# Streaming encoder block on 8 cores: normalisation of x, key products and pooling values in one stream

## The chip, the cores and the metric

The kernel runs on 8 cores of one Trainium2 chip. Each core computes one of the 8 sequences of the batch; the cores exchange nothing. The metric is the device time of the slowest core, in microseconds (us), as the median of several runs. Engines are called PE (TensorE, matrix products), ACT (ScalarE), DVE (VectorE), POOL (GpSimd) and SP (the queue that issues loads).

## The reference

Each core gets x (2048 rows of 1024) and puts 16 learned meta rows in front, so there are T = 2064 rows. Cut to what the change touches:

```
u  = rmsnorm(h, norm1_g)                       # h: meta rows and x
q, c, iq, ik, iw, pv, gates = split(u @ w_in)  # 512|128|256|32|8|512|2048 columns
c  = rmsnorm(c, kv_norm_g)                     # latent keys, 128 wide
attn = sparse_attention(q, iq, iw * IDX_SCALE, c, ik)   # top 256 keys by an index score
pool = multiscale_pool(pv)                     # 4 groups of 128 channels, windows 2, 4, 8, 16:
                                               # trailing mean minus the value, then w_pool, scale
merged = sigmoid(gA) * (attn @ w_a) + sigmoid(gB) * (pool @ w_b)
h  = h + merged @ w_out;  h = h + moe(rmsnorm(h, norm2_g));  out = rmsnorm(h)
```

All of the change lies in what is computed before the attention: u, c, iw, ik, iq, pv and the pooling.

## The kernel before, in words

The program is one list of operations for each engine, in the order in which the Python code calls `pg.op` and `pg.dma`. Every engine works off its own list strictly in that order. Each operation names the buffers that it reads and writes, and the class `Prog` turns these into waits on semaphores: nothing is reordered later, so the order of the calls is the order on each engine. The first stretch, up to the first `pg.barrier()`, is written as phases one behind the other.

1. **Norm of x** (loop over `tiles`: the meta rows, tile -1, then 16 tiles of 128 rows). SP loads a tile into one of four buffers. `rmsnorm_to_uT` squares and sums it on ACT (L433), takes the root on ACT (L436) and the reciprocal on DVE (L439), scales it on DVE (L440, into `xn`, two buffers), and transposes it on PE in 8 pieces (L449, PSUM banks 0 and 1). The copy of the transposed tile into `uT` (ACT, L457) is called one tile later, so ACT squares the next tile meanwhile.
2. **Key products** (`p2a_f1` and its two later parts, by tiles): PE multiplies `uT` of the tile by 136 columns of weights (8 matrix products, L522, banks 2 and 3): 128 latent keys and 8 index weights. ACT squares the keys (L529) and takes the root (L532); DVE does reciprocal, scaling and index weights (L535, L536, L541). One tile later PE transposes the keys (L547), and ACT copies them out (L552).
3. **Pooling values** (`p2b_pv(m)`, m = 3, 2, 1, 0): channel group m for the blocks of 16, 512, 512, 512 and 512 rows. One value group is 8 matrix products (L623) and one copy from PSUM to `pvT` on ACT (L582). The banks rotate over all 8.
4. **Pooling sums** (`p3_chain(g)`): g+1 steps of doubling. In each step POOL adds the first 1024 rows (L639) and DVE the rest (L642), and each half needs both halves of the step before; then DVE takes the mean minus the value (L652) with two short pieces for the first rows (L656, L659) into one of two buffers `dT`. `p3_chain(3)` is called after value group 2, `p3_chain(2)` after group 1.
5. **Index keys and queries** (`p2b_ik`, L592, 5 blocks; `p2b_iq`, L608, 12 groups of 8 products), each copied by ACT.
6. **Pooling products** (`p3_mm(g)`: 4 products, L667, and 4 copies on ACT, L671). `p3_chain(1)` needs the `dT` buffer that `p3_mm(3)` reads, and `p3_chain(0)` the one that `p3_mm(2)` reads; both products are called after all index products.

Then comes the barrier, on which all engines wait; behind it POOL issues the load of `w_uk` (the first L122 row after it) and clears buffers (L721), and the attention begins. What follows the barrier is the same in both kernels.

POOL's queue also fetches the weights, cast to bf16 on the way: `wsmall` (128 columns), `wsmall2` (8), `wik` three times (32 columns each, into three places side by side), `w_iq2` (256), `wslab` (512) and `wpool`, in this order, right at the start.

The lines that carry the order:

```
for j in tiles:                      # norm of x
    ...
    bk_ = rmsnorm_to_uT(xt4[k], [B('xt', k)], rows, col0, gbc[0], B('gbc', 0), j)
...
for j in tiles:                      # key products, after all tiles
    f2 = p2a_f1(j)
...
p2b_pv(3); p2b_pv(2); p3_chain(3); p2b_pv(1); p3_chain(2); p2b_pv(0)
p2b_ik(); p2b_iq(); p3_mm(3); p3_mm(2); p3_chain(1); p3_mm(1); p3_chain(0); p3_mm(0)
```

## Time and profile before

| what | us |
|---|---|
| median of 3 runs | 1480.84 (1477.96 to 1563.48) |
| the profiled execution | 1482.97 |
| its span on the slowest core (core 7) | 1481.4 |
| the other cores of the profiled execution | 1438.8 to 1471.0 |
| busy of core 7: PE, DVE, ACT, POOL | 1064.9, 886.1, 748.1, 318.1 |

The profile is of one execution, on its slowest core. The profiled execution's own time is 1.6 us more than the span from first to last instruction, and 2.1 us more than the median. Times in rows are us from the start of the span. An engine's row in the timeline has its start, its duration, the engine, the source line, the operation, what it writes and reads, and, in brackets, how long the engine had stood idle before it and what released it. PEld is the loading of weights into PE, one for each matrix product.

### The profile page before, as it was taken

What the parts mean: (1) busy time and instruction counts of PE and PEld (TensorE: products, weight loads), DVE (VectorE), ACT (ScalarE), POOL (GpSimd) and SP (SyncE); (2) the same over time, 40 slices, a digit from 0 to 9 for tenths busy, and PEclk for the clock granted to TensorE, in tenths of its full rate; (3) what the DMA queues carried; (4) which work ended last, traced back from release to release, by engine and by line L of the source; (5) the groups of instructions that cost most, each with busy time, mean ns of one, the idle gap of its engine ahead of it and who ended that gap; (6) DMA issues with size and microseconds to landing.
All of it is one profiled execution on the core that took longest, in us unless ns stands there. A gap on an engine that the chain in (4) does not pass through costs nothing.

```text
span 1481.4 us, 23028 instructions; the slowest of 8 cores (1438.8 to 1481.4 us)
## 1 busy us (share of the span) xinstructions
PE 1064.9 (72%) x6606; PEld 549.1 (37%) x6606; DVE 886.1 (60%) x1804; ACT 748.1 (50%) x1395; POOL 318.1 (21%) x318
## 2 busy tenths in 40 slices
PE   2589667787888889999866999988457777683000
PEld 1445223333333334444432444444244545451000
DVE  3434699899999999999731433446622332233195
ACT  5733666676877678888753222256123332332042
POOL 2025402122121122122112000012033334321022
PEclk9999577889989999999987999999669999997555
DMA  9402554564748557886576310055258899884682
GB/s 195 116 1 30 61 61 58 72 88 71 110 65 104 78 77 109 113 109 97 96 98 116 60 24 6 1 166 198 71 168 269 284 287 295 288 274 157 198 298 100
DMA packets 76322, 187.73 MB, mean 127 GB/s; under 512 B 18792, under 2 KB 30568, under 8 KB 72096
## 3 DMA queue, kind: packets, MB, share of 16 engines
q0 software_dynamic: 51264, 87.55, 36.3%
q1 hardware_dynamic: 20320, 86.05, 18.9%
q10 hardware_dynamic: 4608, 12.58, 2.2%
q8 instruction: 59, 0.97, 0.3%
q14 instruction: 71, 0.58, 0.1%
HBM read 223.33 MB, written 88.08 MB: 210 GB/s over the span
## 4 chain that ended last, share of the span: by engine, by line
PE 42%; DVE 21%; issue 15%; ACT 8%; DMA 7%; another core or an unknown queue 3%; POOL 1%; DVEq 0%; ACTq 0%; SPq 0%; POOLq 0%
DVE R L961 11%; PE ps L1214 8%; PE ps L1607 5%; PE ps L1631 4%; DMA R<-y_rows 3%; PE ps L1309 2%; PE ps L623 2%; PE ps L823 2%; PE ps L1198 2%; PE ps L1206 2%; PE ps L1038 2%; PE ps L1020 2%; PE ps L1021 2%; PE ps L1039 2%
## 5 line engine op out<-in xcount | busy, mean ns | idle before, releaser
L961 DVE TENSOR_SCALAR_CACHE_REDUCE R<-R 128x272 bf16<-128x272 f32 (+14 forms) x240 | 342.2, 1426 | 11.6 <-DVE R L961 0.5
L1024 ACT ACTIVATE R<-ps,R 128x512 bf16<-128x512 f32 x304 | 209.2, 691 | 69.8 <-PE ps L1021 63.1
L813 ACT ACTIVATE R<-ps 128x400 bf16<-128x400 f32 (+14 forms) x352 | 159.2, 512 | 55.9 <-PE ps L808 54.2
L1038 PE MATMUL ps<-R 128*128 128x512 bf16 x304 | 120.9, 398 | 33.5 <-ACT R L1046 32.3
L1050 POOL TENSOR_TENSOR R<-R 128x512 bf16<-128x512 f32 x32 | 40.5, 1267 | 457.5 <-ACT R L1048 362.2
L1020 PE MATMUL ps<-R 128*128 128x512 bf16 x304 | 122.1, 401 | 6.4 <-DVE R L928 3.0
L823 PE MATMUL ps<-R 128*128 128x400 bf16 (+14 forms) x352 | 106.7, 383 | 26.5 <-POOL R L796 16.8
L1021 PE MATMUL ps<-R 128*128 128x512 bf16 x304 | 121.3, 399 | 0.0
L1039 PE MATMUL ps<-R 128*128 128x512 bf16 x304 | 120.4, 396 | 0.0
L1214 PE MATMUL ps<-R 128*128 128x512 bf16 x512 | 116.7, 381 | 0.0
L1607 PE MATMUL ps<-R 128*128 128x192 bf16 x1024 | 94.2, 253 | 0.7 <-DVE R L1593 0.7
L808 PE MATMUL ps<-R 32*128 32x400 bf16 (+14 forms) x352 | 71.7, 371 | 30.5 <-DVE R L928 14.7
L1607 PEld LDWEIGHTS ps<-R 128*128 128x128 bf16 x1024 | 86.5, 101 | 16.4 <-issue 15.9
L1631 PE MATMUL ps<-R 128*128 128x512 bf16 (+1 forms) x256 | 81.3, 433 | 11.7 <-ACT R L1640 10.2
L1614 DVE TENSOR_TENSOR R<-R,ps 128x384 bf16<-128x384 f32 x32 | 17.7, 554 | 110.3 <-remote 55.7
L130 POOL DMA_INDIRECT y_rows<-R x48 | 47.6, 993 | 158.8 <-DVE R L1643 87.5
L1226 DVE TENSOR_TENSOR R<-R,ps 128x512 f32<-128x512 f32 x32 | 22.0, 688 | 93.7 <-ACT R L1222 93.7
L1581 PE MATMUL ps<-R 128*128 128x128 bf16 x384 | 31.8, 238 | 60.8 <-ACT R L1589 51.0
L1214 PEld LDWEIGHTS ps<-R 128*128 128x128 bf16 x512 | 50.4, 98 | 61.5 <-issue 1.9
L1640 ACT COPY R<-ps 128x512 f32<-128x512 f32 x64 | 37.3, 583 | 63.1 <-PE ps L1631 60.7
L1643 DVE COPY R<-ps 128x512 f32<-128x512 f32 x64 | 44.1, 689 | 39.4 <-PE ps L1631 37.7
L1222 ACT ACTIVATE R<-ps 128x512 f32<-128x512 f32 x32 | 19.1, 597 | 88.8 <-PE ps L1214 88.8
(211 smaller groups left out, 1927.7 us busy)
## 6 DMA issues: line engine op xcount, KB each, us to landing
R<-expert_bf SPq DMA_DIRECT2D x32, 1024.0 KB
R<-x SPq DMA_DIRECT2D x32, 512.0 KB
expert_bf<-w_eg POOLq DMA_DIRECT2D x32, 512.0 KB
expert_bf<-w_eu POOLq DMA_DIRECT2D x32, 512.0 KB
expert_bf<-w_ed POOLq DMA_DIRECT2D x32, 512.0 KB
R<-expert_bf SPq DMA_DIRECT2D x32, 512.0 KB
R<-y_rows SPq DMA_DIRECT2D x16, 1024.0 KB
out<-R ACTq DMA_DIRECT2D x16, 512.0 KB, 2.9
```

What stands on the lines that cost most here:

```text
L808: pg.op('pe', lambda e, bx=bx, g_=g_, a_=a_: e.matmul(banks[bx][:, 0:n], lhsT=iqT_all[32 * a_:32 * a_ + 32, g_, 128 * j:128 * (j + 1)], rh ...
L813: pg.op('act', lambda e, bx=bx, ri=ri: e.activation(out=rbuf[ri][:, 0:n], in_=banks[bx][:, 0:n], func=AF.Relu), reads=[PB[bx]], writes=[B( ...
L823: pg.op('pe', lambda e, h=h, ri=ri: e.matmul(banks[PSS][:, 0:n], lhsT=dg[:, h, :], rhs=rbuf[ri][:, 0:n], start=(h == 0), stop=(h == 7)), r ...
L961: pg.op('dve', lambda e: e.tensor_scalar(out=junkbf[:, 0:S], in0=sc[:, 0:S], scalar1=mids[:, n_ - 1:n_], scalar2=None, op0=ALU.is_ge, op1= ...
L1020: e.matmul(banks[bl][:, 0:512], lhsT=cnT[:, kc0:kc0 + 128], rhs=qrhs, start=True, stop=False)
L1021: return e.matmul(banks[bl][:, 0:512], lhsT=ident_bf, rhs=mrow, start=False, stop=True)
L1024: pg.op('act', lambda e: e.activation(out=pT[pi], in_=banks[bl][:, 0:512], func=AF.Exp, scale=ATTN_SCALE, bias=negsh[:, par:par + 1]), rea ...
L1038: e.matmul(banks[bO][:, 0:512], lhsT=ckeys[:, i, 0:128], rhs=pT[pi], start=first, stop=last_)
L1039: return e.matmul(banks[bS][:, 0:512], lhsT=ones_bf, rhs=pT[pi], start=first, stop=last_)
L1214: last = e.matmul(banks[bk][:, 0:512], lhsT=wt[:, kc, n4 * 128:(n4 + 1) * 128], rhs=uT[:, kc, c0:c0 + 512], start=(kc == 0), stop=(kc == K ...
L1607: last = e.matmul(banks[bk][:, CAP * fh:CAP * (fh + 1)], lhsT=w[:, c_:c_ + 128], rhs=xt_[:, kc, :], start=(kc == 0), stop=(kc == KC - 1))
L1631: last = e.matmul(banks[bk][lo:hi_, 0:512], lhsT=hd[:, f, t0:t1_], rhs=w[:, 4096 + 1024 * f + 512 * hh:4096 + 1024 * f + 512 * (hh + 1)], ...
```

## The change

Three things change, all ahead of the first barrier.

- **One stream.** One loop over the tiles does the norm of a tile (`take(j)`) and then takes two pieces of work (three from tile 12 on) from a list. A piece is either a key product step `p2a_step(j)` or one value group `p2b_pv(m, bi)`. The pieces of a block of four tiles are put on the list when the tile after the block has been taken, in turn key step, value group, key step, and so on; of the last block first its four value groups, then its four key steps. These last four key steps are called after `p3_chain(3)` and `p3_chain(2)`.
- **Copies and banks of the values.** Value groups use PSUM banks 6 and 7 alone, and two of three are copied by DVE, every third by ACT.
- **Weights and index products.** `wik` is fetched once and copied twice by POOL; it, `w_iq2` and `wpool` are fetched when tile 4 has been called, and the fetch of `wik` names `xn` 0 as read (so it starts when tile 3's scaled rows are there, and the next writer of `xn` 0, tile 5, waits until it has landed). `p2b_iq` is called by its three parts, with `p3_mm(3)`, `p3_chain(1)`, `p3_mm(2)`, `p3_chain(0)` and `p3_mm(1)` between and behind them.

The diff:

```diff
--- before.py
+++ after.py
@@ -475,20 +475,14 @@
 
         xt4 = xt + [ptmp[0][:, 0:D], ptmp[1][:, 0:D]]
         tiles = [-1] + list(range(NT))
-        pend1 = None
-        for j in tiles:
+
+        def take(j):
             rows = 16 if j < 0 else 128
             col0 = 0 if j < 0 else 16 + 128 * j
             k = nxt('xt4', [0, 1, 2, 3])
             src = meta_d if j < 0 else x_d[128 * j:128 * (j + 1), :]
             pg.dma('sp', xt4[k][0:rows], src, writes=[B('xt', k)])
-            if j == 1:
-                late_consts()
-            bk_ = rmsnorm_to_uT(xt4[k], [B('xt', k)], rows, col0, gbc[0], B('gbc', 0), j)
-            if pend1 is not None:
-                pend1()
-            pend1 = bk_
-        pend1()
+            return rmsnorm_to_uT(xt4[k], [B('xt', k)], rows, col0, gbc[0], B('gbc', 0), j)
 
         def uT_bufs(c0, c1):
             res = []
@@ -504,11 +498,15 @@
 
         pg.dma('pool', wsmall[:, :, 0:128], win_p[:, :, 512:640], writes=[B('wsmall')])
         pg.dma('pool', wsmall[:, :, 128:136], win_p[:, :, 928:936], reads=[], writes=[B('wsmall2')])
-        for r_ in range(3):
-            pg.dma('pool', wik[:, :, 32 * r_:32 * r_ + 32], win_p[:, :, 896:928], writes=[B('wik', r_)])
-        pg.dma('pool', w_iq2, win_p[:, :, 640:896], writes=[B('w_iq2')])
         pg.dma('pool', wslab, win_p[:, :, 936:1448], writes=[B('wslab')])
-        pg.dma('pool', wpool, wpool_d.rearrange("g c d -> c g d"), writes=[B('wpool')])
+
+        def late_weights():
+            pg.dma('pool', wik[:, :, 0:32], win_p[:, :, 896:928], reads=[B('xn', 0)], writes=[B('wik', 0)])
+            pg.dma('pool', w_iq2, win_p[:, :, 640:896], writes=[B('w_iq2')])
+            pg.dma('pool', wpool, wpool_d.rearrange("g c d -> c g d"), writes=[B('wpool')])
+            for r_ in (1, 2):
+                pg.op('pool', lambda e, r_=r_: e.tensor_copy(out=wik[:, :, 32 * r_:32 * r_ + 32], in_=wik[:, :, 0:32]),
+                      reads=[B('wik', 0)], writes=[B('wik', r_)])
 
         def p2a_f1(j):
             rows = 16 if j < 0 else 128
@@ -555,17 +553,14 @@
                 return f3
             return f2
 
-        p_f2, p_f3 = None, None
-        for j in tiles:
-            f2 = p2a_f1(j)
-            f3 = p_f2() if p_f2 is not None else None
-            if p_f3 is not None:
-                p_f3()
-            p_f2, p_f3 = f2, f3
-        f3 = p_f2()
-        if p_f3 is not None:
-            p_f3()
-        f3()
+        p2 = [None, None]
+
+        def p2a_step(j):
+            f2 = p2a_f1(j) if j is not None else None
+            f3 = p2[0]() if p2[0] is not None else None
+            if p2[1] is not None:
+                p2[1]()
+            p2[0], p2[1] = f2, f3
 
         blocks = [(0, 16)] + [(16 + 512 * b, 16 + 512 * (b + 1)) for b in range(4)]
         allb = list(range(8))
@@ -595,8 +590,8 @@
                 pg.op('pe', mm, reads=uT_bufs(c0, c1) + [B('wik', 0), B('wik', 1), B('wik', 2)], writes=[PB[bk]])
                 act_evac(ikT[0:96, c0:c1], banks[bk][0:96, 0:n], [PB[bk]], [B('ikT', bi)])
 
-        def p2b_iq():
-            for g in range(3):
+        def p2b_iq(g):
+            if True:
                 M = 96 if g < 2 else 64
                 for b in range(4):
                     bk = nxt('gen', allb)
@@ -612,9 +607,10 @@
                     act_evac(iqT_all[0:M, g, 512 * b:512 * (b + 1)], banks[bk][0:M, 0:512], [PB[bk]],
                              [B('iqT_all', g, b)])
 
-        def p2b_pv(m):
-            for bi, (c0, c1) in enumerate(blocks):
-                bk = nxt('gen', allb)
+        def p2b_pv(m, bi):
+            if True:
+                c0, c1 = blocks[bi]
+                bk = nxt('pvb', [6, 7])
                 n = c1 - c0
 
                 def mm(e, bk=bk, c0=c0, c1=c1, n=n):
@@ -624,7 +620,10 @@
                                         rhs=uT[:, kc, c0:c1], start=(kc == 0), stop=(kc == KC - 1))
                     return last
                 pg.op('pe', mm, reads=uT_bufs(c0, c1) + [B('wslab')], writes=[PB[bk]])
-                act_evac(pvT[:, m, c0:c1], banks[bk][:, 0:n], [PB[bk]], [B('pvT', m)])
+                eng = nxt('pve', ['dve', 'dve', 'act'])
+                fn = (lambda e: e.copy(out=pvT[:, m, c0:c1], in_=banks[bk][:, 0:n])) if eng == 'act' else \
+                    (lambda e: e.tensor_copy(out=pvT[:, m, c0:c1], in_=banks[bk][:, 0:n]))
+                pg.op(eng, fn, reads=[PB[bk]], writes=[B('pvT', m)])
 
         p3_di = {}
 
@@ -675,21 +674,58 @@
 
         W_Q_OFF = 25344
         w_q = carve_at('R3', W_Q_OFF, BF16, [P, KC, 512])
-        p2b_pv(3)
-        p2b_pv(2)
+        work = []
+
+        def queue_block(b):
+            pvs = [lambda m=m: p2b_pv(m, b + 1) for m in (3, 2, 1, 0)]
+            if b == 0:
+                pvs = [lambda m=m: p2b_pv(m, 0) for m in (3, 2, 1, 0)] + pvs
+            pas = [lambda j=j: p2a_step(j) for j in ([-1] if b == 0 else []) + list(range(4 * b, 4 * b + 4))]
+            if b == 3:
+                work.extend(pvs + pas)
+                return
+            while pvs or pas:
+                if pas:
+                    work.append(pas.pop(0))
+                if pvs:
+                    work.append(pvs.pop(0))
+
+        back = None
+        for j in tiles:
+            nb = take(j)
+            if j == 1:
+                late_consts()
+            if j == 4:
+                late_weights()
+            if back is not None:
+                back()
+            back = nb
+            if j >= 4 and j % 4 == 0:
+                queue_block(j // 4 - 1)
+            for _ in range(2 if j < 12 else 3):
+                if work:
+                    work.pop(0)()
+        back()
+        queue_block(3)
+        while len(work) > 4:
+            work.pop(0)()
         p3_chain(3)
-        p2b_pv(1)
         p3_chain(2)
+        for f in work:
+            f()
+        p2a_step(None)
+        p2a_step(None)
         if stop_after >= 4:
             pg.dma('pool', w_q, win_p[:, :, 0:512], writes=[B('w_q'), B('pvT', 3)])
-        p2b_pv(0)
         p2b_ik()
-        p2b_iq()
+        p2b_iq(0)
         p3_mm(3)
+        p3_chain(1)
+        p2b_iq(1)
         p3_mm(2)
-        p3_chain(1)
+        p3_chain(0)
+        p2b_iq(2)
         p3_mm(1)
-        p3_chain(0)
         p3_mm(0)
 
         if stop_after <= 3:
```

What stands in a row on three engines, before and now:

**PE, before: the last two tiles of the norm and the first key products.** An L449 row is the 8 transposes of one tile, and all 17 tiles stand in a row with nothing between them; L522 are the key products of a tile, L547 the transpose of its keys.

```order
L449 MATMUL ps1<-R0 128x128 x8
L449 MATMUL ps0<-R0 128x128 x8
L522 MATMUL ps2<-R2,R0 16x136 x8
L522 MATMUL ps3<-R2,R0 128x136 x8
L547 MATMUL ps4<-R0,R1 128x16
```

**PE, now: the middle of the stream.** L449 transposes tile 9 in the first row and tiles 10 and 11 in the later ones; L619 is a value group (before: L623), L520 are the key products of a tile (before: L522), L545 the transpose of a tile's keys (before: L547).

```order
L449 MATMUL ps0<-R0 128x128 x8
L619 MATMUL ps7<-R0,R2 128x512 x8
L619 MATMUL ps6<-R0,R2 128x512 x8
L449 MATMUL ps1<-R0 128x128 x8
L619 MATMUL ps7<-R0,R2 128x512 x8
L520 MATMUL ps3<-R2,R0 128x136 x8
L545 MATMUL ps4<-R0,R1 128x128
L449 MATMUL ps0<-R0 128x128 x8
L619 MATMUL ps6<-R0,R2 128x512 x8
L520 MATMUL ps2<-R2,R0 128x136 x8
L545 MATMUL ps5<-R0,R1 128x128
```

The key products and the value groups have moved between the transposes of two x tiles. PE can start none of them before it has transposed the x tile that stands ahead of them.

**ACT, before: tile 15 and the first key steps.** L433 squares an x tile, L436 takes the root, L457 copies the transposed tile before it; L529 and L532 square keys and take their root.

```order
L433 ACTIVATE R0<-R0 128x1024
L436 ACTIVATE R0<-R0 128x1
L457 COPY R0<-ps1 128x8x128
L457 COPY R0<-ps0 128x8x128
L529 ACTIVATE R0<-ps2 16x128
L532 ACTIVATE R0<-R0 16x1
```

**ACT, now: tiles 9 to 11 of the stream.** L527 squares the keys of a tile (before: L529), L530 takes their root (before: L532), L550 copies transposed keys (before: L552), L624 is ACT's copy of a value group.

```order
L433 ACTIVATE R0<-R2 128x1024
L436 ACTIVATE R0<-R0 128x1
L457 COPY R0<-ps1 128x8x128
L624 COPY R3<-ps7 128x512
L433 ACTIVATE R0<-R2 128x1024
L436 ACTIVATE R0<-R0 128x1
L457 COPY R0<-ps0 128x8x128
L527 ACTIVATE R0<-ps3 128x128
L530 ACTIVATE R0<-R0 128x1
L550 COPY R1<-ps5 128x128
L433 ACTIVATE R0<-R0 128x1024
```

The squares of keys have moved between those of two x tiles: ACT squares the next x tile only after the copy of a value group or the squares of keys, which come from PE.

**DVE, at the end of the stream, before.** L642, L652, L656 and L659 are `p3_chain`; first group 3, then group 2, then group 1.

```order
L652 SCALAR_TENSOR_TENSOR R<-R 128x2057
L656 TENSOR_TENSOR R<-R 128x7
L659 TENSOR_TENSOR R<-R 128x7
L642 TENSOR_TENSOR R<-R 128x1040 x2
L652 SCALAR_TENSOR_TENSOR R<-R 128x2061
```

**DVE, now.** L625 is DVE's copy of a value group; L641, L651, L655 and L658 are the lines of `p3_chain`; L533, L534 and L539 are DVE's part of a key step (before: L535, L536, L541).

```order
L625 COPY R<-ps 128x512 x4
L641 TENSOR_TENSOR R<-R 128x1040 x4
L651 SCALAR_TENSOR_TENSOR R<-R 128x2049
L655 TENSOR_TENSOR R<-R 128x15
L658 TENSOR_TENSOR R<-R 128x15
L641 TENSOR_TENSOR R<-R 128x1040 x3
L651 SCALAR_TENSOR_TENSOR R<-R 128x2057
L655 TENSOR_TENSOR R<-R 128x7
L658 TENSOR_TENSOR R<-R 128x7
L533 RECIPROCAL R<-R 128x1
L534 SCALAR_TENSOR_TENSOR R<-ps,R 128x128
L539 TENSOR_SCALAR R<-ps 128x8
```

DVE's parts of the last four key steps (four times the last three rows) now stand behind the whole of groups 3 and 2 of the pooling sums. On PE the transposes of those keys (L545) stand ahead of all index products.

## Rows read from the trace of the kernel before

**Rows 1.** Windows by stage: us, busy us of each engine (instructions), PEclk, DMA share, GB/s.

```profile
0.00:61.50 61.50, 17.25 (x136) 13.78 (x136) 25.05 (x35) 39.53 (x68) 8.12 (x16) 1.00 0.92 187
61.50:89.50 28.00, 20.08 (x156) 15.80 (x155) 11.29 (x50) 14.54 (x68) 0.00 (x0) 1.00 0.00 1
89.50:119.80 30.30, 30.30 (x168) 13.98 (x167) 11.16 (x9) 9.42 (x21) 17.89 (x11) 1.00 0.00 1
119.80:147.70 27.90, 27.90 (x133) 15.22 (x131) 10.11 (x7) 9.37 (x17) 14.50 (x11) 1.00 0.29 39
147.70:160.15 12.45, 4.82 (x17) 1.59 (x16) 6.27 (x7) 9.89 (x17) 0.58 (x1) 0.77 0.00 0
```

**Rows 2.** Timeline, norm of x: tile 4's transposes, then one whole tile.

```profile
29.32 1.05 PE L449 MATMUL ps<-R 128*128 128x128 bf16 x8 [1.32 <-ACT R L457]
...
43.18 1.06 ACT L433 ACTIVATE R<-R 128x1024 bf16<-128x1024 f32 x1
...
44.42 0.29 ACT L436 ACTIVATE R<-R 128x1 f32<-128x1 f32 x1
44.82 0.16 DVE L439 RECIPROCAL R<-R 128x1 f32<-128x1 f32 x1 [0.79 <-ACT R L436]
45.15 1.28 DVE L440 SCALAR_TENSOR_TENSOR R<-R 128x1024 bf16<-128x1024 f32 x1 [0.17 <-DVE R L439]
...
46.69 1.04 PE L449 MATMUL ps<-R 128*128 128x128 bf16 x8 [1.47 <-DVE R L440]
```

**Rows 3.** Timeline, key products: one tile on PE and ACT.

```profile
86.58 1.06 PE L522 MATMUL ps<-R 128*128 128x136 bf16 x8
...
87.75 0.28 ACT L529 ACTIVATE R<-ps 128x128 bf16<-128x128 f32 x1 [1.13 <-PE ps L522]
...
88.21 0.29 ACT L532 ACTIVATE R<-R 128x1 f32<-128x1 f32 x1
88.41 0.41 ACT L552 COPY R<-ps 128x128 bf16<-128x128 bf16 x2
```

**Rows 4.** Timeline, values: first weight loads of PE, then copies of value groups.

```profile
92.22 0.15 PEld L623 LDWEIGHTS ps<-R 128*128 128x128 bf16 x1 [0.28 <-issue]
92.65 0.15 PEld L623 LDWEIGHTS ps<-R 128*128 128x128 bf16 x1 [0.28 <-issue]
93.03 26.17 PEld L623 LDWEIGHTS ps<-R 128*128 128x128 bf16 x143 [0.23 <-issue]
...
95.01 0.59 ACT L582 COPY R<-ps 128x512 f32<-128x512 f32 x1 [1.14 <-PE ps L623]
96.74 0.59 ACT L582 COPY R<-ps 128x512 f32<-128x512 f32 x1 [1.14 <-PE ps L623]
```

**Rows 5.** Timeline, pooling sums of groups 3 and 2.

```profile
99.20 2.95 POOL L639 TENSOR_TENSOR R<-R 128x1023 f32<-128x1023 f32 x1 [89.70 <-ACT R L582]
...
102.65 1.24 DVE L642 TENSOR_TENSOR R<-R 128x1040 f32<-128x1040 f32 x1 [2.26 <-POOL R L645]
...
125.58 2.30 DVE L652 SCALAR_TENSOR_TENSOR R<-R 128x2057 bf16<-128x2057 f32 x1 [2.17 <-POOL R L645]
...
...
129.76 0.17 DVE L659 TENSOR_TENSOR R<-R 128x7 bf16<-128x7 f32 x1
```

**Rows 6.** Timeline around the barrier.

```profile
156.53 2.42 ACT L671 ACTIVATE R<-ps,R 128x512 bf16<-128x512 f32 x4 [1.17 <-PE ps L667]
...
159.57 0.59 POOL L122 DMA_DIRECT2D R<-w_uk  x1 [22.64 <-ACT R L671]
```

**Rows 7.** Groups by line, whole span: DVE's copy of 512 columns from PSUM.

```profile
L1643 DVE COPY R<-ps 128x512 f32<-128x512 f32 x64 | 44.1, 689 | 39.4 <-PE ps L1631 37.7 <-ACT R L1640 1.7
```

**Rows 8.** DMA queues, 10 to 20 us: packets, MB, share of 16 engines.

```profile
DMA packets 5630, 1.72 MB, mean 172 GB/s; under 512 B 5026, under 2 KB 5350, under 8 KB 5630
...
q0 software_dynamic: 4219, 0.43, 80.4%
```

**Rows 9.** Waits, 0 to 160 us: engine and line, what it waited for, us, times, longest.

```profile
ACT R L433 <- DMA R<-x: 4.4, 4, 2.1
```

## The prediction

> **What bounds the kernel now.** I read the windows by stage first, since the change touches only what lies ahead of the first barrier [rows 1]. There the reader sees four phases that end at about 61.5, 89.5, 119.8 and 147.7 us, and a tail until the barrier. In the first phase PE is busy 17 of 61.5 us and ACT 40; in the second no engine is busy all the time; in the third and fourth PE is busy throughout. So about 44 us of PE's time in the first phase look free, and the change wants to fill them. The barrier is passed at 159.57, when POOL issues the load of w_uk after its wait for ACT's last pooling copies [rows 6]. All that follows is the same in both kernels and starts from the barrier, so I price the change as the shift of that moment.
>
> Next I read the timeline of one x tile and of one key step [rows 2, 3], since in an in-order program it is the latency between engines, not their busy time, that a new order can bring onto the path.
>
> **The start is unchanged.** Tiles -1 to 4 come in the same order as before, so tile 4's transposes start at 29.3 [rows 2].
>
> **The loop over tiles 5 to 15.** Before, a tile costs ACT its own work of some 2.7 us, because ACT squares a tile while DVE and PE work on the one before it. Now ACT's list has, behind the squares of a tile, the squares of keys whose product PE may start only after it has transposed this same x tile. So the engines wait for each other once round. From transposes to transposes: transposes 1.05 [rows 2]; key products until ACT squares the keys 1.17 (86.58 to 87.75), until the root 0.46, until the copy 0.20, two copies take 0.41, so one until the next tile's squares 0.20 [rows 3]; squares to root 1.24 (43.18 to 44.42), root to reciprocal 0.40, reciprocal to scaling 0.33, and scaling to transposes 1.54 (45.15 to 46.69) [rows 2]. The sum is 6.59; scaling to transposes is at best 1.28 and a short wait, 1.4, so I take 6.45 for a round without a value group.
>
> A value group takes 1.73 us (96.74 less 95.01), when PE runs at the higher level of its clock [rows 4]. By the order of the lists, in the rounds from tile 9 to tile 14 one value group stands between the transposes and what ACT waits for (either ahead of the key products on PE, or copied by ACT); the other groups fall into the 4 us in which PE waits for the next scaled tile, and cost nothing. The round of tile 9 has no key step and that of tile 13 has two, which about cancels. DVE's copies of value groups, 0.69 us each [rows 7], fall into its waits and cost nothing as long as the round is longer than DVE's 3 us of work in it.
>
> The fetch of wik once instead of three times: from 10 to 20 us the software queue moved 4219 packets in 80.4% of the 16 engines' time, 30 ns of an engine each [rows 8]. Two fetches less are 2048 packets, 3.9 us of all 16. Before, ACT waited for x 4.4 us in all [rows 9], so at most 4.4 us can be won, and some 1 to 2 if the waits shrink with the load. Against it stands that tile 5's scaling now waits until the late fetch of wik has landed. It is issued at some 27 us, and wslab is ahead of it; in the old order the software queue was emptied by 51 us, in the new one with half of its bytes ahead I take 34.5. Tile 5's scaling would come at 34.4 by the loop alone, so I take both terms as nothing, with -3 and +17 (51 less 34) as ends.
>
> Tile 15's transposes so start at 29.3 + 11 x 6.45 + 6 x 1.73 = 110.6.
>
> **The end of the values.** From there PE does the transposes, 1.05, two key steps of 1.06 + 0.27 and three value groups of 1.73 until group 3 of the last block is there: 8.9. Its copy takes 0.69, so POOL begins the pooling sums at 120.2. Before it was at 99.2 [rows 5].
>
> **The sums of groups 3 and 2, and what is now queued behind them.** Before, they took POOL and DVE from 99.2 to DVE's last piece at 129.9: 30.7 us [rows 5]. Now DVE must first copy the last value groups, which PE ends 5.2 us later than group 3, so DVE's first piece comes after some 125.8; POOL's second step waits for it (before, it started 3.5 us after the first [rows 5]), which adds 3.2. DVE is free at 154.1. In DVE's list the last four key steps stand behind these sums, and in PE's list the transposes of these keys stand ahead of the index keys. PE does one or two key products more and then idles for over 25 us. Before, the sums ran beside 28 us of index products and nobody waited for them. This is the dearest term.
>
> From 154.1: four key steps, one behind the other, of which two still need their products on PE: 4.7 (two bank waits; a key step took 28.0 / 17 = 1.65 before [rows 1]). Index keys and queries 27.9 [rows 1]. Pooling products of groups 3 and 2 between them, 8 x 0.22 = 1.8. The products of groups 1 and 0 come last with 8 copies on ACT of 2.42 / 4 = 0.6 [rows 6], 5.4 with the first wait. The barrier comes at 193.9. The sums of groups 1 and 0 run beside the index products now, which saves 12.45 less 5.4 of the old tail [rows 1]; that is within the sum.
>
> **The clock of PE.** The granted clock stands at 1.00 in all these windows [rows 1], but the first loads of the values are 0.43 us apart until 93.03 (92.22, 92.65), which is 512 columns at 1.2 GHz, the lower level, and then a group takes 1.73, which is the higher one [rows 4]. Ahead of it PE was busy 72% of 28 us with key products of 136 columns, and stayed low [rows 1]. In the new stream PE waits some 4 us in each round, so its value groups may run at 3.41 (8 x 0.427) instead of 1.73. Twelve of them lie on the path (six in the rounds, two around the last key steps, four of the last block): nothing if all are at the higher level, 12 x 1.68 = 20.2 if all are at the lower. I take half, 10.1, since the last five stand in a row and those in the rounds start after a wait. The index keys after the long idle time start low too: 7 products at 0.43 instead of 0.21, 1.5.
>
> The Trainium skill ("TensorE: Matmul & The Clock Gate", Part 1) says that an array that has idled runs at half rate, with matrix products N / 1.2 GHz apart, and N / 2.4 GHz once it has been busy; the first loads of the values agree. By its rule every group in the rounds starts low, and the sum would be the upper one.
>
> **The sum.** Barrier at 193.9 + 10.1 + 1.5 = 205.5 instead of 159.6, 45.9 later. The profiled execution took 1482.97, so 1528.9; that execution lay 2.1 above the median of the runs, so I forecast 1527 us, 3% more.
>
> **Rivals.**
> 1. *The stream runs at ACT's pace.* If ACT didn't wait in each round, it would have 39.5 + 14.5 us of work [rows 1], 4 of copies of values and 4.4 of waits for x after its start at 9.1: about 72, less 3 for the last key steps. The sums would start at 71 instead of 120 and the barrier would come at 71 + 33.9 + 4.7 + 27.9 + 1.8 + 5.4 = 145, 15 earlier than before: 1466 us, within 2%, not slower. For it speaks how idle PE is; against it the two lists, in which ACT's squares of keys and PE's transposes wait for each other. It decides when a round averages below some 3.3 us instead of 6.45 (35 us over 11 rounds); faster by over 2% would need DVE's queue not to hold up PE as well, and gives 1466 less 25 = 1441.
> 2. *The sums don't hold up PE.* If the last four key steps went through before the sums, 25 us of the idle time would go: 1502. For it speaks that POOL and DVE only start when all values are copied; against it DVE's list.
> 3. *The high clock.* All value groups at 1.73: 1480.8 + 34.3 = 1515 or, with the index start, 1517. For it: dense value groups did run so [rows 4]. Its opposite, all low: 1537.
> 4. *The late weights.* If wik lands when the software queue was empty before, tile 5 comes 17 later: 1544.
>
> **How the numbers follow.** The forecast with either clock: 0.80. The late weights: 0.06. The sums not in the way: 0.05. ACT's pace: 0.07, and with both gains 0.02. The likeliest case spans 1515 to 1537 by the clock; with -3 from x and what the waits may be smaller it reaches to 1508, with a part of the late weights to 1548. A measurement of this kernel tells about 2% from no change, which is 1511 above and 1451 below. Below 1451 lies only the last case: 0.02. Within 2% lie ACT's pace and the sums not in the way: 0.12. Slower: 0.86.
>
> **What would show it.** In the profile after: x tiles' transposes 6 to 9 us apart from tile 5 on; ACT idle before the squares of keys and PE idle before the transposes of x in every round; POOL's first sum at 120 to 135; an idle stretch of PE of 25 us or more before the index keys, ended by DVE; the load of w_uk at some 205. It would be wrong if the rounds were near 4 us, or if PE went on to the index keys while POOL sums, or if what follows the barrier took another time than before, which I count as nothing because no operation there differs.

## The result, and the profile after

| what | before | after |
|---|---|---|
| median | 1479.41 us (4 runs) | 1529.0 us (4 runs, 1523.08 to 1542.2) |
| ratio, 95% interval | | 1.0351 [1.0264, 1.0437] |
| the profiled execution | 1482.97 | 1523.08 |
| its span, slowest core (core 7 in both) | 1481.4 | 1521.4 |
| load of w_uk behind the barrier, core 7 | 159.57 | 202.75 |
| from there to the end of the span | 1321.8 | 1318.65 |

The change makes the kernel slower by 3.5%; a second measurement of the same kernel gave 1.0288 [1.0254, 1.0323]. The last two lines say where: the barrier comes 43.2 us later, and what follows takes 3.2 us less. The medians take all runs; the ratios leave out runs in a slower state that some executions of every kernel on 8 cores show. The windows by stage of the kernel after (core 7; columns as in [rows 1]):

```profile
0.00:38.80 38.80, 7.24 (x64) 5.80 (x65) 11.19 (x18) 16.82 (x31) 8.11 (x16) 1.00 1.04 184
38.80:116.00 77.20, 43.19 (x274) 26.65 (x274) 25.99 (x59) 32.04 (x83) 0.02 (x1) 0.85 0.20 55
116.00:128.50 12.50, 12.11 (x75) 6.25 (x76) 3.42 (x9) 3.62 (x11) 2.07 (x2) 1.00 0.00 1
128.50:163.90 35.40, 3.93 (x38) 3.10 (x36) 20.36 (x27) 3.43 (x17) 24.27 (x15) 0.55 0.19 28
163.90:196.70 32.80, 32.80 (x145) 17.58 (x144) 10.29 (x9) 13.55 (x25) 4.97 (x4) 0.91 0.02 3
196.70:203.30 6.60, 1.94 (x9) 0.70 (x8) 0.00 (x0) 5.18 (x9) 0.55 (x1) 1.00 0.00 1
```

Two rows hold the loss. In the stream of tiles 5 to 15 (second row) no engine is busy for even 60% of 77 us. In the fourth row PE does 3.93 us of work in 35.4, while POOL and DVE add up. Before, PE was busy throughout while the sums of groups 3 and 2 ran [rows 1].

The timeline of the stream: PE from tile 4's transposes on, and ACT in one round.

```profile
32.40 1.05 PE L449 MATMUL ps<-R 128*128 128x128 bf16 x8 [2.03 <-DVE R L440]
35.87 0.36 PE L619 MATMUL ps<-R 128*128 128x16 bf16 x8 [1.41 <-DMA R<-w_in]
38.81 1.05 PE L449 MATMUL ps<-R 128*128 128x128 bf16 x8 [2.59 <-DVE R L440]
...
51.13 1.05 PE L449 MATMUL ps<-R 128*128 128x128 bf16 x8 [3.92 <-DVE R L440]
...
53.18 0.28 ACT L527 ACTIVATE R<-ps 128x128 bf16<-128x128 f32 x1 [2.95 <-PE ps L520]
53.65 0.29 ACT L530 ACTIVATE R<-R 128x1 f32<-128x1 f32 x1
53.99 1.06 ACT L433 ACTIVATE R<-R 128x1024 bf16<-128x1024 f32 x1
55.23 0.29 ACT L436 ACTIVATE R<-R 128x1 f32<-128x1 f32 x1
...
57.43 1.05 PE L449 MATMUL ps<-R 128*128 128x128 bf16 x8 [4.04 <-DVE R L440]
...
88.92 1.05 PE L449 MATMUL ps<-R 128*128 128x128 bf16 x8 [4.18 <-DVE R L440]
89.76 3.62 PE L619 MATMUL ps<-R 128*128 128x512 bf16 x8
...
98.73 0.68 PE L449 MATMUL ps<-R 128*128 128x128 bf16 x8 [2.40 <-DVE R L440]
99.78 1.89 PE L619 MATMUL ps<-R 128*128 128x512 bf16 x8
...
116.05 0.68 PE L449 MATMUL ps<-R 128*128 128x128 bf16 x8 [2.42 <-DVE R L440]
```

Follow the brackets of one round. At 51.13 PE has waited 3.92 us for DVE's scaling. ACT then waits 2.95 us for PE's key products, squares the keys (53.18), takes their root (53.65), and only then squares the next x tile (53.99), whose scaled rows PE waits 4.04 us for until 57.43. Each engine waits for the other once in each round of 6.30 us. The last rows show the two levels of PE's clock: 8 products of 512 columns in 3.62 us or in 1.89.

The timeline of the pooling sums and the way to the barrier, on all engines:

```profile
124.41 1.89 POOL L638 TENSOR_TENSOR R<-R 128x1023 f32<-128x1023 f32 x1 [85.59 <-DVE R L625]
129.43 2.58 DVE L641 TENSOR_TENSOR R<-R 128x1040 f32<-128x1040 f32 x2
130.93 2.82 POOL L638 TENSOR_TENSOR R<-R 128x1022 f32<-128x1022 f32 x1 [4.31 <-ACT R L550]
...
158.78 0.17 DVE L658 TENSOR_TENSOR R<-R 128x7 bf16<-128x7 f32 x1
159.16 0.35 DVE L534 SCALAR_TENSOR_TENSOR R<-ps,R 128x128 bf16<-128x128 f32 x1
159.66 0.26 PE L545 MATMUL ps<-R 128*128 128x128 bf16 x1 [30.01 <-DVE R L534]
...
163.96 10.28 PE L587 MATMUL ps<-R 128*96 128x16 bf16 x40
...
196.74 1.90 PE L666 MATMUL ps<-R 128*128 128x512 bf16 x8
202.75 0.60 POOL L122 DMA_DIRECT2D R<-w_uk  x1 [32.20 <-ACT R L670]
```

DVE ends the last piece of the sums at 158.95, and the scaling of keys behind it in its list (L534, 0.35 us) is what PE had waited 30.01 us for. The waits of the kernel after, 0 to 205 us (engine and line, what it waited for: us, times, longest):

```profile
PE ps L449 <- DVE R L440: 50.0, 16, 5.4
PE ps L545 <- DVE R L534: 31.5, 3, 30.0
PE ps L619 <- DMA R<-w_in: 1.4, 1, 1.4
```

The first two lines hold the two losses; of the 50.0 us of the first line, 36.6 are the waits from tile 5 on, the rest belongs to the start. ACT's waits for x are 2.0 to 6.1 us by core, 4.3 on the mean of the eight, as before (3.2 to 5.2, mean 4.3). One more wait is not on core 7 but on six of the others, here on DVE of core 1, ahead of tile 5's scaling:

```profile
35.57 1.38 DVE L440 SCALAR_TENSOR_TENSOR R<-R 128x1024 bf16<-128x1024 f32 x1 [2.16 <-DMA R<-w_in]
```

It is the wait for the late fetch of wik, 1.06 to 3.04 us long on these six cores.

### The profile page after: what moved, and what is told of

Its sections match the earlier page's. It is cut to its first block, busy times and chain, and to the rows that moved or that the text cites. A ratio compares the mean times of both kernels' runs of the same rounds, so it can differ in the third digit from the quotient of the medians.

```text
span 1521.4 us, 22944 instructions; the slowest of 8 cores (1494.1 to 1521.4 us)
## 1 busy us (share of the span) xinstructions
PE 1058.4 (70%) x6606; PEld 544.3 (36%) x6606; DVE 889.5 (58%) x1818; ACT 739.9 (49%) x1381; POOL 316.9 (21%) x318
## 4 chain that ended last, share of the span: by engine, by line
PE 42%; DVE 20%; issue 13%; ACT 9%; DMA 7%; another core or an unknown queue 3%; POOL 3%; ACTq 0%; DVEq 0%; SPq 0%; POOLq 0%
DVE R L997 10%; PE ps L1250 7%; PE ps L1643 5%; PE ps L1667 4%; DMA R<-y_rows 3%; PE ps L859 2%; PE ps L619 2%; PE ps L1234 2%; PE ps L1074 2%; PE ps L1242 2%; PE ps L1056 2%; PE ps L1057 2%; PE ps L1075 2%; PE ps L1345 2%
## 5 line engine op out<-in xcount | busy, mean ns | idle before, releaser
L997 DVE TENSOR_SCALAR_CACHE_REDUCE R<-R 128x272 bf16<-128x272 f32 (+14 forms) x240 | 342.1, 1425 | 11.6 <-DVE R L997 0.5
L1074 PE MATMUL ps<-R 128*128 128x512 bf16 x304 | 118.9, 391 | 33.9 <-ACT R L1082 32.4
L1056 PE MATMUL ps<-R 128*128 128x512 bf16 x304 | 119.7, 394 | 8.0 <-DVE R L1003 3.9
L1057 PE MATMUL ps<-R 128*128 128x512 bf16 x304 | 119.1, 392 | 0.0
L1075 PE MATMUL ps<-R 128*128 128x512 bf16 x304 | 118.7, 390 | 0.0
L1250 PE MATMUL ps<-R 128*128 128x512 bf16 x512 | 115.7, 379 | 0.0
L1667 PE MATMUL ps<-R 128*128 128x512 bf16 (+1 forms) x256 | 84.4, 449 | 11.2 <-ACT R L1676 10.4
L844 PE MATMUL ps<-R 32*128 32x400 bf16 (+14 forms) x352 | 72.1, 371 | 28.4 <-DVE R L964 13.6
L1345 PE MATMUL ps<-R 128*128 128x512 bf16 x256 | 60.3, 391 | 3.6 <-DVE R L1266 2.6
```

The costliest lines, as they stand in the source:

```text
L997: pg.op('dve', lambda e: e.tensor_scalar(out=junkbf[:, 0:S], in0=sc[:, 0:S], scalar1=mids[:, n_ - 1:n_], scalar2=None, op0=ALU.is_ge, op1= ...
L1056: e.matmul(banks[bl][:, 0:512], lhsT=cnT[:, kc0:kc0 + 128], rhs=qrhs, start=True, stop=False)
L1057: return e.matmul(banks[bl][:, 0:512], lhsT=ident_bf, rhs=mrow, start=False, stop=True)
L1074: e.matmul(banks[bO][:, 0:512], lhsT=ckeys[:, i, 0:128], rhs=pT[pi], start=first, stop=last_)
L1075: return e.matmul(banks[bS][:, 0:512], lhsT=ones_bf, rhs=pT[pi], start=first, stop=last_)
L1250: last = e.matmul(banks[bk][:, 0:512], lhsT=wt[:, kc, n4 * 128:(n4 + 1) * 128], rhs=uT[:, kc, c0:c0 + 512], start=(kc == 0), stop=(kc == K ...
```

## The experiments

Since everything behind the barrier is common to all kernels, each run has a second measure, which varies less than the time: when POOL issues the load of w_uk. In us, over the 8 cores of the profiled execution, with the ratio to the kernel before and its 95% interval:

| kernel | w_uk, mean (lowest to highest) | median | ratio |
|---|---|---|---|
| before | 159.1 (157.1 to 161.0) | 1479.41 | 1 |
| after | 203.0 (200.5 to 205.5) | 1529.0 | 1.0351 [1.0264, 1.0437] |
| e9_after_again | 204.8 (202.8 to 207.5) | 1530.84 | 1.0288 [1.0254, 1.0323] |
| e1_keys_first | 181.4 (177.8 to 183.6) | 1510.16 | 1.0123 [1.0078, 1.0167] |
| e2_turn_later | 159.2 (156.5 to 162.6) | 1484.33 | 0.999 [0.9957, 1.0022] |
| e3_both_moves | 137.8 (135.7 to 141.1) | 1462.85 | 0.985 [0.981, 0.989] |
| e11_both_again | 138.4 (135.8 to 140.8) | 1465.8 | 0.9856 [0.9811, 0.99] |
| e7_alternate_last | 134.3 (130.9 to 136.4) | 1466.63 | 0.9891 [0.9788, 0.9993] |
| e12_sums_sooner | 136.2 (132.9 to 140.5) | 1461.37 | 0.9821 [0.9787, 0.9856] |
| e4_index_mixed | 155.5 (154.9 to 156.4) | 1482.28 | 0.9963 [0.9928, 0.9999] |
| e5_wik_once | 160.1 (156.4 to 163.0) | 1485.23 | 0.998 [0.9945, 1.0015] |
| e6_filler | 195.9 (191.9 to 200.2) | 1532.0 | 1.0347 [1.03, 1.0395] |
| e10_filler_again | 196.0 (192.2 to 198.7) | 1512.59 | 1.017 [1.0129, 1.0211] |
| e8_old_weights | 210.7 (208.3 to 211.9) | 1548.83 | 1.0445 [1.0347, 1.0543] |

e1 to e4 ran beside each other on one chip, then e5 to e8, then e9 to e12. The ratios take the kernel before on the same chip, so they compare better than the medians do. For 11 of the 13 kernels behind the first row the shift of the barrier, as a part of 1480.8 us, lies within the ratio's interval, so the barrier does price the change; the exceptions are e6_filler and e10_filler_again, one on each side.

**e1_keys_first.** The change, but the last key steps stand ahead of the sums.

```diff
         queue_block(3)
-        while len(work) > 4:
-            work.pop(0)()
-        p3_chain(3)
-        p3_chain(2)
         for f in work:
             f()
         p2a_step(None)
         p2a_step(None)
+        p3_chain(3)
+        p3_chain(2)
```

> The changed kernel with one move: the last four key steps are called ahead of the pooling sums of groups 3 and 2, and not behind them. If PE's 30 us of waiting in front of the index keys come from DVE's queue, as I hold, the wait in front of the last keys' transposes falls from 30 us to below 2 us, the sums run beside the index products, and the load of w_uk comes 18 to 26 us sooner than at 202.8 (some 7 us of key steps now lie ahead of the sums): 1503 to 1511 us. If PE waited for something else (the index weights, banks), the wait stays and the time is 1529 within 5. The slow rounds of the stream stay as they are in both cases (8 to 9 us for a tile).

The barrier comes 21.6 us sooner than in the kernel after, as expected (18 to 26), and the ratio falls by 1.65 points from that of e9_after_again (24 us) and by 2.28 from that of the first measurement (34 us), both on other chips. The waits (core 0, 0 to 185 us):

```profile
PE ps L449 <- DVE R L440: 51.4, 16, 4.6
PE ps L666 <- DVE R L658: 5.1, 1, 5.1
PE ps L545 <- DVE R L534: 0.6, 1, 0.6
```

PE's wait of 30 us has gone. A new one of 5.1 us stands at the pooling products of group 2 (L666), which now overtake the sums. The rounds of the stream are what they were (first line). So DVE's list was the cause of this loss, and it was worth 22 us and not 30, because the index products start sooner but meet the sums: on core 0 they begin 18.4 us behind tile 15's transposes (135.86, 117.43) instead of 47.9 (core 7 of the kernel after), but from there to the load of w_uk it takes 46.3 us instead of 38.8. Behind its wait of 5.1 us PE is also slower for a while: the last 32 index products take 8.90 us (167.23) where they took 7.09 in the kernel after.

**e2_turn_later.** The change, but a tile's transposes are put in PE's list behind the two or three pieces of work of the round, so that ACT's squares of keys no longer need the transposes of the x tile that ACT has squared just before them.

```diff
-            pg.op('pe', tps, reads=[B('xn', k), B('ident_bf')], writes=[PB[bk]])
+            def turn():
+                pg.op('pe', tps, reads=[B('xn', k), B('ident_bf')], writes=[PB[bk]])
...
-            nb = take(j)
+            turn, nb = take(j)
...
             for _ in range(2 if j < 12 else 3):
                 if work:
                     work.pop(0)()
+            turn()
```

> The changed kernel with one move: in each round the transposes of the x tile are issued on PE behind the two or three pieces of work instead of ahead of them. If the rounds are long because ACT's squares of keys and PE's transposes wait for each other, as I hold, a round falls from 8.4 us (mean of tiles 5 to 15) to 4.5 to 6, PE hardly waits in it, and the w_uk load comes 27 to 40 us sooner than at 202.8: 1490 to 1503 us. The wait of 30 us behind DVE's sums stays. If the rounds were bound by the lower clock of PE alone, or by the loads of x, they would stay above 7.5 us and the time above 1515.

The barrier comes 43.8 us sooner than after the change, at the place of the kernel before, and the ratio is 0.999. That is more than I expected (27 to 40). The windows of the kernel after (core 7) and of this one (core 3), each over its stream from 39 us on:

```profile
39.00:128.00 89.00, 54.61 (x346) 32.49 (x345) 29.41 (x68) 35.66 (x94) 2.07 (x2) 0.87 0.17 47
```

```profile
39.00:86.00 47.00, 43.42 (x323) 26.62 (x323) 27.28 (x64) 32.64 (x89) 2.07 (x2) 1.00 0.25 77
```

Nearly the same work (323 of 346 products, 89 of 94 operations of ACT) takes 47 us and not 89, and PE is busy for 92% of it. Its timeline (PE, core 3), one late round and tile 15's transposes:

```profile
67.34 0.67 PE L449 MATMUL ps<-R 128*128 128x128 bf16 x8
67.85 1.89 PE L623 MATMUL ps<-R 128*128 128x512 bf16 x8
...
71.83 0.65 PE L449 MATMUL ps<-R 128*128 128x128 bf16 x8
75.86 0.67 PE L449 MATMUL ps<-R 128*128 128x128 bf16 x8
```

No bracket stands behind these transposes: the scaled tile is there before PE comes to it (two earlier tiles of this stretch, at 42.99 and 59.50, waited 1.70 and 1.43 us). From tile 4 (32.67) to tile 15 a round takes 3.93 us on the mean, against 7.60 in the kernel after (32.40 to 116.05). That is less than the 4.5 to 6 that I had expected, and a part of it is the clock: value groups take 1.89 us from 53 us on, none 3.62. On the mean of the cores tile 15's transposes come 39.8 us sooner than in the kernel after (76.5 for 116.3), from there to POOL's first sum it is 3.3 us shorter (5.1 for 8.4), since PE now does the pieces of the last round ahead of the transposes, and the rest is 0.7. The other loss is untouched, as it should be (waits, core 3):

```profile
PE ps L549 <- DVE R L538: 31.8, 4, 29.8
PE ps L449 <- DVE R L440: 11.1, 5, 4.4
```

**e3_both_moves**, and again as **e11_both_again**. Both edits at once.

```diff
-        p3_chain(3)
-        p3_chain(2)
...
         p2a_step(None)
         p2a_step(None)
+        p3_chain(3)
+        p3_chain(2)
...
+            turn()
```

> Both moves of the two kernels before. If the two waits are independent terms of the sum, the gains add up: the w_uk load at 145 to 158 us, 1472 to 1484 us, which is no slower than the kernel before the change. If one wait only hides behind the other, the time stays within 5 us of the better of the two single moves.

> The kernel with both moves, once more, in 5 rounds beside the next kernel. Ratio to the kernel before 0.983 to 0.988.

The barrier comes 65.2 us sooner than after the change; the single edits gave 21.6 and 43.8, 65.4 together. So they are two separate losses. At 137.8 the barrier also lies ahead of the 145 to 158 that I had expected, by what e2 gave more than I had thought. The ratio is 0.985, and 0.9856 on another chip, both intervals clear of 1: with both mended, the idea of the change gains 1.5%. What is left in it, by the timeline of POOL and DVE and by the waits (core 1):

```profile
81.16 1.89 POOL L642 TENSOR_TENSOR R<-R 128x1023 f32<-128x1023 f32 x1 [42.00 <-DVE R L629]
91.02 2.58 DVE L645 TENSOR_TENSOR R<-R 128x1040 f32<-128x1040 f32 x2
92.40 2.95 POOL L642 TENSOR_TENSOR R<-R 128x1022 f32<-128x1022 f32 x1 [9.03 <-ACT R L581]
```

```profile
PE ps L623 <- DMA R<-w_in: 6.4, 1, 6.4
PE ps L670 <- DVE R L662: 5.1, 2, 4.8
```

POOL begins at 81.16 but waits 9.03 us before its second step, because DVE's half of the first step now stands behind copies of values and the last key steps in DVE's list and begins only at 91.02. (The bracket names an ACT cast of the index keys that ended at nearly the same moment, but the second step reads nothing of it.) PE waits 6.4 us for the value weights, wslab, ahead of its first value group, and 4.8 us for the sums of group 2.

**e12_sums_sooner.** e3 with the last block in another order: the four key steps first, then the value groups, copied by ACT alone, with the sums of group 3 behind the first two.

```diff
-                eng = nxt('pve', ['dve', 'dve', 'act'])
+                eng = 'act' if bi == 4 else nxt('pve', ['dve', 'dve', 'act'])
...
-                work.extend(pvs + pas)
+                work.extend(pas + [lambda: p2a_step(None)] + pvs[:1] + [lambda: p2a_step(None)] + pvs[1:2]
+                            + [lambda: p3_chain(3)] + pvs[2:])
...
-        p2a_step(None)
-        p2a_step(None)
-        p3_chain(3)
         p3_chain(2)
```

> The kernel with both moves, and the last block in another order: its four key steps first, then its value groups, all four copied by ACT, with the sums of group 3 called right behind value groups 3 and 2. POOL's first sum then starts 4 to 6 us sooner, the key steps no longer stand between values and index products, and PE's waits for the sums (4.8 us in front of group 2's pooling products) shrink. The w_uk load 2 to 5 us sooner than in the kernel with both moves (136), 1458 against 1463 us. If PE's own work sets the end by now, under 1 us.

The timeline of POOL and PE (core 1):

```profile
85.22 2.88 POOL L642 TENSOR_TENSOR R<-R 128x1023 f32<-128x1023 f32 x1 [49.18 <-ACT R L628]
88.57 2.95 POOL L642 TENSOR_TENSOR R<-R 128x1022 f32<-128x1022 f32 x1
...
116.29 1.86 PE L670 MATMUL ps<-R 128*128 128x512 bf16 x4 [4.45 <-DVE R L662]
```

The gap of 9 us has gone. But POOL begins later, not 4 to 6 us sooner as expected: at 88.2 on the mean of the cores, against 82.2 in e11_both_again, and its second step comes at 91.6 instead of 93.4, 1.9 us sooner. (Core 1 alone, 88.57 against the 92.40 above, flatters it, since its stream ended sooner too.) PE still waits 4.45 us ahead of group 2, and the barrier wins 2.2 us of the expected 2 to 5. This is the fastest of the kernels, 1.8% faster than before. Its lead over e11_both_again (0.9856) lies within the intervals, with 2 us at the barrier.

**e7_alternate_last.** e3, with the pieces of the last block in turn like those of the others.

```diff
-            if b == 3:
-                work.extend(pvs + pas)
-                return
```

> The kernel with both moves, and the last block's four key steps in turn with its value groups like those of the other blocks, instead of all behind them. In the kernel with both moves PE waited 0.7 to 1.2 us four times between these key steps. I hold that the value groups cover these waits, so the index keys start some 3 us sooner than at 91.3, and the w_uk load comes 2 to 4 us sooner than at 136: 1459 against 1463. If the pooling sums set the end (PE waited 4.8 us for the sums of group 2), less of it arrives: 0 to 2 us.

The barrier comes 3.5 us sooner than in e3, as expected (2 to 4) and the soonest of all, but PE waits longer for the sums: L670 <- DVE R L662 is 10.1 us in four waits on core 2, against 5.1 in two on core 1 of e3. The time doesn't show the gain: the ratio is 0.9891 with an interval from 0.9788 to 0.9993, which holds e3's ratio.

**e4_index_mixed.** The kernel before, with the index products among the pooling sums as in the change.

```diff
         p2b_ik()
-        p2b_iq()
+        p2b_iq(0)
         p3_mm(3)
-        p3_mm(2)
         p3_chain(1)
-        p3_mm(1)
+        p2b_iq(1)
+        p3_mm(2)
         p3_chain(0)
+        p2b_iq(2)
+        p3_mm(1)
         p3_mm(0)
```

> The kernel before, with the one part of the change that I counted as a gain: index queries by their three parts with the pooling products and sums of groups 1 and 0 between them. I hold that it removes 7 us of the tail: the w_uk load at 152 to 154 instead of 159.6, 1472 to 1475 us against 1480. If the tail is bound by ACT's copies instead, the load stays at 158 or later and the time does not change.

The barrier comes 3.6 us sooner, half of what I expected. PE's timeline (core 3) shows why:

```profile
120.39 7.43 PE L592 MATMUL ps<-R 128*96 128x16 bf16 x40
...
134.57 1.03 PE L667 MATMUL ps<-R 128*128 128x512 bf16 x4
...
150.32 1.90 PE L667 MATMUL ps<-R 128*128 128x512 bf16 x8
```

The tail from the last index product to the barrier is 6.07 us (150.32 to 156.39) instead of 11.87 (147.70 to 159.57 [rows 1, 6]). But the pooling products that it lost stand among the index products now, whose stretch lasts 29.9 us (from 120.39) instead of 28.2 (119.53 to 147.73, core 7 before). This part of the change is good for a few tenths of a per cent.

**e5_wik_once.** The kernel before, with wik fetched once, in its old place, and copied twice by POOL.

```diff
-        for r_ in range(3):
-            pg.dma('pool', wik[:, :, 32 * r_:32 * r_ + 32], win_p[:, :, 896:928], writes=[B('wik', r_)])
+        pg.dma('pool', wik[:, :, 0:32], win_p[:, :, 896:928], writes=[B('wik', 0)])
...
+        for r_ in (1, 2):
+            pg.op('pool', lambda e, r_=r_: e.tensor_copy(out=wik[:, :, 32 * r_:32 * r_ + 32], in_=wik[:, :, 0:32]),
+                  reads=[B('wik', 0)], writes=[B('wik', r_)])
```

> The kernel before, with the one part of the change that touches the fetches alone: the index key weights fetched once, in the same place of the queue, and copied twice by POOL. 2048 packets of 64 to 128 bytes fewer, some 30 ns of an engine each, are 3.9 us of all 16 engines. I hold that ACT's waits for x, 4.4 us in all, shrink by 1 to 3 us and the w_uk load comes 1 to 3 us sooner than at 159.6; the median is the same within the measurement. If these packets did not hold up x, the load stays within 0.5 us.

I had expected 1 to 3 us. The barrier comes at 160.1 on the mean, no sooner, and the ratio is 0.998 [0.9945, 1.0015]. On every core the software queue moved 5776 packets in the first 61 us instead of 7856, and from 10 to 20 us 3210 on the mean of the cores instead of 3819 (on core 7 2983 instead of the 4219 of [rows 8]). And yet ACT waits for x 2.1 to 6.5 us by core, 4.5 on the mean, not less than the 4.3 of before. Tile 4's transposes come at 28.9 on the mean of the cores, against 28.0. So the wait did not shrink with the number of packets.

**e8_old_weights.** The change, with the weights fetched as before it.

```diff
+        for r_ in range(3):
+            pg.dma('pool', wik[:, :, 32 * r_:32 * r_ + 32], win_p[:, :, 896:928], writes=[B('wik', r_)])
+        pg.dma('pool', w_iq2, win_p[:, :, 640:896], writes=[B('w_iq2')])
         pg.dma('pool', wslab, win_p[:, :, 936:1448], writes=[B('wslab')])
...
-            if j == 4:
-                late_weights()
```

> The changed kernel with the weights fetched as in the kernel before: index key weights three times, then index query weights, then wslab, all at the start. The value weights then land behind 3.9 us of small packets and 0.5 MB: PE's first value group, which waited until 35.9, waits until 45 to 51, and with it the whole stream behind it: 10 to 15 us later, 1538 to 1545 us. If the order of the fetches did not matter, the time stays within 5 us of 1529; if it was a loss (x loaded later: tile 4's transposes at 32.4 instead of 29.3), it falls by 3.

PE's timeline (core 3):

```profile
28.58 1.05 PE L449 MATMUL ps<-R 128*128 128x128 bf16 x8 [1.21 <-DVE R L440]
43.22 0.36 PE L615 MATMUL ps<-R 128*128 128x16 bf16 x8 [12.59 <-DMA R<-w_in]
45.49 1.04 PE L449 MATMUL ps<-R 128*128 128x128 bf16 x8 [1.91 <-DVE R L440]
```

The first value group waits 12.59 us for wslab, and tile 5's transposes come at 45.5 on the mean of the cores instead of 38.1. The barrier is 6 to 8 us later than after the change, less than the 10 to 15 that I had expected, since wslab landed before the 45 to 51 of my estimate. So the order of the fetches is what this part of the change is worth, in a kernel that wants the values so early. It also shows the price: tile 4's transposes come at 28.4 on the mean here, at 30.1 after the change (29.9 in e9_after_again), 28.0 before. The other kernels bear this out: e1, e6 and e10, with the order of the change, have tile 4 at 29.7, 29.7 and 30.2, and e4, with the old order, at 28.4. With wslab fetched sooner, the tiles of x come 1.5 to 2 us later.

**e6_filler**, and again as **e10_filler_again.** The change, with 6 products of 512 columns more on PE in each of 9 rounds; nobody reads them.

```diff
+        def fill():
...
+                for i in range(6):
+                    last = e.matmul(banks[bk][:, 0:512], lhsT=wslab[:, i, 0:128], rhs=uT[:, i, 16:528],
+                                    start=(i == 0), stop=(i == 5))
...
+            if 6 <= j < NT - 1:
+                fill()
```

> The changed kernel with 6 products of 512 columns more in each round of tiles 6 to 14, into the bank of the next value group, whose result nobody reads: they fill a part of the 4 us in which PE waits for the next scaled tile. If the lower level of PE's clock in the value groups costs 6 to 10 us of the stream, as I hold after reading its trace (groups of 3.6 us beside groups of 1.9), the groups run at 1.9 us all through and tile 15's transposes come 5 to 9 us sooner than at 116, in spite of the added work: 1520 to 1524 us. If the clock costs nothing on the path, or the added products run past the wait, the time stays or grows by up to 5 us.

> The changed kernel itself, as a control on the chip of the next runs, since the added products of the run before moved the w_uk load by 4 to 8 us in the traces and left the median where it was. I expect 1.03 to 1.04 of the kernel before, and the w_uk load at 202 to 206.

> The changed kernel with the added products in PE's waits, once more, beside the changed kernel itself. If the 4 to 8 us that the stream wins by the higher level of the clock reach the end, its ratio lies 0.3 to 0.5% below that of the control. If what follows the barrier gives them back, the two ratios agree within 0.2%.

The windows of 39 to 116 us (core 7), of the kernel after and then of e6_filler:

```profile
39.00:116.00 77.00, 43.00 (x274) 26.45 (x272) 25.99 (x59) 32.04 (x83) 0.00 (x0) 0.84 0.20 55
```

```profile
39.00:116.00 77.00, 54.62 (x364) 31.50 (x365) 27.62 (x63) 33.58 (x90) 1.14 (x1) 0.93 0.19 52
```

The granted clock rises from 0.84 to 0.93 (on the eight cores 0.82 to 0.89 without the filler, 0.91 to 0.96 with it, two runs of each), and with more products on PE the barrier comes 7 to 9 us sooner. Of this the stream has all: tile 15's transposes come at 109.8 on the mean of the cores instead of 116.3, and at 109.9 in e10 instead of e9's 118.5. The edit only adds work and waits to PE's list, so this gain is the clock's, and it is the least that the low level costs in the stream, since the clock is not at 1.00 here either: against what I had expected, not all value groups ran at 1.9 us (on core 7 three took 2.81 to 3.07). The times don't agree with each other: e6's ratio (1.0347) is no better than that of the kernel after, e10's is 1.2 points (17 us) better than its neighbour e9's, where I had expected 0.3 to 0.5 and the barrier moved by 9 us. How much of the stream's gain reaches the end stays open.

## Why the prediction was right

I had forecast 1527 us, and 1529.0 was measured. The terms, with the kernel after on core 7 (plain terms and clock put together where they lie in one stretch):

| step | predicted | measured |
|---|---|---|
| tile 4's transposes | 29.3 | 32.40 |
| tile 4 to tile 15 | 81.3 + 5.0 clock | 83.65 |
| tile 15 to POOL's first sum | 9.6 | 8.36 (124.41) |
| clock of the last six value groups | 5.0 | 0 |
| first sum to DVE free | 33.9 | 34.54 (158.95) |
| last key steps | 4.7 | 5.01 (163.96) |
| index and pooling products | 29.7 + 1.5 clock | 32.8 |
| to the load of w_uk | 5.4 | 6.0 |
| sum | 205.5 | 202.75 |

- *The rounds.* This is the step that carried the forecast most, and it held. Three plain rounds from 38.81 to 57.43 take 6.21 us each; I had 6.45, with each link as in the rows of before. e2 shows that the cause was the one named, the place of the transposes in PE's list: without it a round takes 3.93 us.
- *DVE's queue in front of PE.* PE idles 30.01 us, where I had over 25, and the sums take 34.54 for 33.9. e1 shows the cause. Rival 2 priced the opposite at 1502; e1's ratio on 1480.84 gives 1499.
- *The clock.* The mechanism was right, the size not. From tile 8 to tile 15 the stream took 58.62 us; seven plain rounds are 43.4 and six value groups 10.4, so by this subtraction 4.8 are the clock's. The last six groups, for which I had 5.0 more, all ran at 1.89 us. For the index keys I had 1.5, but their 40 products took 10.28 us instead of the 7.43 of e4's: 2.85. In all 7.7 for 11.6, between the two ends of rival 3. The 4.8 is what the value groups took more; the plain rounds ran at the low level themselves (transposes 1.05 us, not 0.68), so the whole cost is higher, at least the 7 to 9 us of e6 and e10. The granted clock read 1.00 in the windows of before up to 147.7 us, but 0.85 in that of the stream.
- *The fetches taken as nothing.* This term was mis-sized, and the step "the start is unchanged" was false: it looked at the order of the tiles and not at wslab, which is now fetched ahead of other weights. Tile 4's transposes came 3.1 us later than I had them on core 7, 2.2 on the mean of the cores. The runs show where most of it comes from: fewer packets win nothing (e5), and wslab's place ahead costs x 1.5 to 2 us (e8). Where tile 4 came early, the late wik then held up tile 5's scaling (the row of core 1 above, 2.16 us); on core 7 it did not (4 to 5 in 6.41 us, a plain round). I had tile 5 at 35.75; it came at 35.9 to 40.0, 38.1 on the mean. The 3 us of this term lie between my ends of -3 and +17.
- *The tail.* 6.0 us for 5.4, and the pooling products in between as in e4.

The errors have both signs: the start, the sums, the key steps, the index products and the tail came out 6.2 us too low together, the stream, the way to the first sum and the last groups' clock 8.9 too high. So part of the closeness is luck; the two terms that make the loss, rounds of over 6 us and an idle PE of 30 us, are not. The barrier came 2.7 us sooner than forecast and the rest took 3.2 less than in the kernel before, but the profiled execution (1523.08) lay 5.9 below the median of the runs, where I had taken it 2 above.

By the rule of the Trainium skill that I weighed ("TensorE: Matmul & The Clock Gate", Part 1), every value group in the rounds would have started low, and the sum would have been 10 us higher. The trace shows both: behind waits of 4.18, 4.18 and 4.25 us of PE (tiles 11, 12 and 14) the group took 3.62, behind waits of 2.40, 2.40 and 2.42 (tiles 10, 13 and 15) it took 1.89. The same page's section on oscillation describes a loop in which every pass starts low; this trace agrees for three of these six rounds, with a granted clock of 0.85 over the stream.

Rival 1, ACT's pace, was false for this order of the lists; e2's order comes near it, with rounds of 3.93 us where the rival wanted 3.3 and POOL's first sum at 81.5 on the mean where it had 71. Rival 4, late weights, cost 1 to 3 us on six cores and not 17; e8 shows how far it can go: with the old order of fetches the first value group comes at 43.22.

## What to carry to other kernels

Before merging two in-order loops, write out one round as a chain of links (who waits for whom, with the durations of the rows): idle time of an engine is only to be had if no operation that another engine needs next stands behind its own wait. Then look, in the list of every engine, at what short operation stands behind a long chain, and who waits for it; moving two calls by a few lines was worth 44 and 22 us here, with the same work done. What the Trainium skill advises ("Perfetto Trace Analysis", Optimization Strategy), to interleave stretches with different limits, made this kernel 3% slower in one order and 1.5% faster in another.
